# A two-block transformer forward on one core: first-layer score products over 128 rows, and the opening transfers in another order

## The chip, the cores and the metric

One core of a Trainium2 chip runs the whole program. The metric is the device time in microseconds (us). Engines: PE is TensorE (its matmuls), PEld its weight loads, DVE is VectorE, ACT ScalarE, POOL GpSimd, SP SyncE, which here only issues transfers.

## What is computed

The reference runs two blocks over 512 tokens of width 1024, in float32. The change lies in the first block. It projects the normed rows `hn` with `w_in` and has four groups of four attention heads, each head 64 wide; their results are gated, projected with `w_out` and added to `x`. The second block (sparse attention, a gated MLP mixer, a SwiGLU) follows.

```python
hn = rms_norm(x, norm_gain)
proj = jnp.einsum('btd,de->bte', hn, w_in)
...
o_fox = forgetting_attention(rms_norm(to_heads(fq, FOX_HEADS), fox_qk_gain[0]), ...)
o_moba = moba_attention(rms_norm(to_heads(mq, MOBA_HEADS), moba_qk_gain[0]), ...)
o_sb = stick_breaking_attention(to_heads(sq, SB_HEADS), ...)
o_swa = swa_sink_attention(rms_norm(to_heads(wq, SWA_HEADS), swa_qk_gain[0]), ...)
...
return x + jnp.einsum('bte,ed->btd', y, w_out)
```

Every head needs the product of its queries and keys, a contraction over 64 numbers: `jnp.einsum('bhqd,bhkd->bhqk', q_i, k)`. The biases that depend on the distance of a query and a key come from tables (`rel_bias`, `rel_bias_2`) by a one-hot product.

## The kernel before

One timeline, a Python list that `make_timeline` writes, sets the order on all engines: each engine walks the list and emits its share of each step, with semaphores between them. The large projections are cut into chunks of at most 512 columns and eight steps of 128 contraction rows. Such a step is called a tick here; it is twelve matmuls (`product`, L1038: four token tiles by three partial products, since each operand is split into a high and a low part). ACT makes the high part of a weight tile (L1425), POOL the low part (L2154), four tiles ahead, in a ring of six. A float32 matmul stands in the profile as two records, an fp32r one as one.

Between the ticks `at(tick, ...)` and `flush` put the attention of the first block: `("S", name, h, g)` is a group of score products of head `h` (PE L1246, then DVE L1933, then the exponential on ACT L1559), `T` its transposes (L1261), `O` its product with the values (L1286), `Z` and `F` the same for the stick-breaking heads `sb` (L1299, L1314). Behind each score segment of `fox` and `sb` stands a 128-row bf16 matmul that adds the mask (L1251, L1301). `fox` has its scores from tick 18, `moba` from 31, `sb` from 45, `swa` from 60.

Queries and keys reach the score products through `qa`, `qb` and `qt`: DVE squares and sums a token tile (L1835 to L1837), POOL takes the power (L2177), DVE scales (L1842), PE transposes four blocks into the bank `TR` (L1214), and DVE copies that bank, two heads per 128 rows, into `qkT1` (L1861, or L1858 for `sb`). The bank `TR` is also where `T` writes, and `T` waits until the copy has freed it. A head's q is then the upper or the lower 64 rows:

```python
e = 64 * (h % 2)
return qkT1[e:e + 64, KINDS1[name] % 2, h // 2, :]
```

The opening: SP loads the first tile of `x`, the gain, the identity, five table transfers, the other tiles of `x`, two groups of weights (L886, groups of four weight tiles, each loaded when the group two before it is split), and then twelve small constants. DVE and POOL multiply by the gain (L1675, L2162), PE transposes (L1112), ACT and DVE make the high and low parts (L1441, L1770). The distance rows (L1047, `distance_rows`) are four float32 matmuls of 33 rows by 8 columns of weights against 512, 512, 512 and 128 columns, and stand before the transposes of the last token tile. `rows_out` on DVE (L1655) copies them out; `setup` (L1637 to L1645) converts the constants. SP stores them, replicates each to 128 rows in DRAM and reads them back skewed as biases.

Of the kernel before, what the change touches and what calls it, by code (L numbers as in the profile page):

```python
# [14 lines left out]
P = 128  # L15
# [125 lines left out]
def make_timeline(first, n_slots):  # L141
# [129 lines left out]
    for t in range(NT):  # L271
# [122 lines left out]
    for t in range(NT):  # L394
        tl.extend([("sq", "ffn", t), ("yf", t, 0), ("ms", "ffn", t), ("yf", t, 1), ("post", "ffn", t)])
    return tl


def hybrid_two_block_kernel(nc, a, c, out):
# [22 lines left out]
    with ExitStack() as ctx:  # L422
# [35 lines left out]
        qkT1 = at("qkT1", 161, [2, 4, SEQ])  # L458
# [8 lines left out]
        hot_cmp = at("hot_cmp", 179, [1024])  # L467
        rows = at("rows", 199, [1664])
# [116 lines left out]
        hot_r = sem("cmp_hots_copied")  # L585
        gains_done = sem("gains_multiplied")
# [13 lines left out]
        qn_done = sem("qk_normed")  # L600
        s_cmp = sem("cmp_hots_landed")
# [260 lines left out]
        def _(sp):  # L862
# [53 lines left out]
            def replicate_rows():  # L916
                sp.wait_ge(s_rows, 48)
                for lo, n in ((0, 4), (8, 8)):
                    for h in range(lo, lo + n):
                        sp.dma_start(rep_d[h], rows_d[h:h + 1, :].broadcast_to([P, 640])).then_inc(s_rep, 16)  # L920
# [7 lines left out]
            def load_bias1():  # L928
                sp.wait_ge(s_rep, 16 * 16)
                for h in range(4):  # L930
                    skewed(bias_moba[:, h, :], rep_d, h, 512, 640).then_inc(s_bias1, 16)
                for h in range(4):
                    skewed(bias_swa[:, h, :], repb_d, h, 256, 384).then_inc(s_bias1, 16)

            def load_bias2():

                sp.wait_ge(tr_in, nth["F", 3, 2] + 1)
                sp.wait_ge(sp_done, 4)
                for h in range(8):
                    skewed(bias_t5[:, h, :], rep_d, 8 + h, 512, 640).then_inc(s_bias2, 16)  # L940

            def load_hot_cmp():

                sp.wait_ge(sc_out, nth["S", "moba", 3, 2] + 1)
# [45 lines left out]
            def load_gain(n, name, pre):  # L990
# [12 lines left out]
                index["out1", 0, 0]: [lambda: load_gain(0, "norm_mix_pre_2", (gx_pool, NT)),  # L1003
# [1201 lines left out]
```

## Time and profile before

| | us |
|---|---|
| median of 3 runs | 1060.28 (1058.92 to 1060.36) |
| the profiled execution | 1059.54 |
| its span, from the first to the last instruction | 1057.4 |
| PE busy | 998.2 (94% of the span) |
| DVE, ACT, POOL busy | 435.3, 390.3, 382.8 |
| chain that ended last, PE's share | 80% |

The profiled execution is 0.74 us below the median and 2.1 us above its own span, which is what lies before and after the first and last instruction. A row of the trace gives the start, the time, the engine, the line of the kernel, the operation, its tile, how many instructions were merged in the row, and in brackets how long the engine sat idle before and what ended that. For PE the form begins with rows*columns of the array, as 64*128. Matmuls overlap: what a matmul costs is read from one start to the next.

### The profile page before, as it was taken

What the parts mean: (1) busy time and instruction counts of PE and PEld (TensorE: products, weight loads), DVE (VectorE), ACT (ScalarE), POOL (GpSimd) and SP (SyncE); (2) the same over time, 40 slices, a digit from 0 to 9 for tenths busy, and PEclk for the clock granted to TensorE, in tenths of its full rate; (3) what the DMA queues carried; (4) which work ended last, traced back from release to release, by engine and by line L of the source; (5) the groups of instructions that cost most, each with busy time, mean ns of one, the idle gap of its engine ahead of it and who ended that gap; (6) DMA issues with size and microseconds to landing.
All of it is one profiled execution on the core that took longest, in us unless ns stands there. A gap on an engine that the chain in (4) does not pass through costs nothing.

```text
span 1057.4 us, 13172 instructions
## 1 busy us (share of the span) xinstructions
PE 998.2 (94%) x5055; PEld 816.7 (77%) x5055; DVE 435.3 (41%) x931; ACT 390.3 (37%) x724; POOL 382.8 (36%) x303
## 2 busy tenths in 40 slices
PE   6979999999998999989988889899999999999997
PEld 3867777776877887888877888787888888888886
DVE  3462532339655544527467756371000110132224
ACT  4232333334735324224546444443222232333332
POOL 4461422235121533223230004444544354444442
PEclk9989999999999999999999999999999999999999
DMA  6652121122115242052130002124332323223222
GB/s 227 194 186 49 41 80 41 40 81 65 41 40 199 81 155 67 22 179 81 40 120 21 1 2 80 41 80 111 125 114 80 120 80 102 98 82 117 80 80 80
DMA packets 69309, 93.06 MB, mean 88 GB/s; under 512 B 10348, under 2 KB 47761, under 8 KB 69248
## 3 DMA queue, kind: packets, MB, share of 16 engines
q1 hardware_dynamic: 69248, 92.23, 27.3%
q8 instruction: 40, 0.66, 0.3%
q14 instruction: 21, 0.17, 0.1%
HBM read 90.09 MB, written 6.85 MB: 92 GB/s over the span
## 4 chain that ended last, share of the span: by engine, by line
PE 80%; DVE 10%; issue 3%; DMA 2%; ACT 2%; POOL 1%; SPq 0%; DVEq 0%; POOLq 0%; ACTq 0%
PE psum L1038 60%; PE psum L1286 5%; PE psum L1246 4%; PE psum L1261 2%; PE psum L1338 1%; PE psum L1112 1%; POOL st L2177 1%; PE psum L1214 1%; DVE prob L1933 1%; DMA r_scratch<-st 1%; PE psum L1314 1%; DMA RAW<-in_w_gate_up_dram 1%; DVE sq L1835 1%; PE psum L1299 1%; DVE R L1741 1%
## 5 line engine op out<-in xcount | busy, mean ns | idle before, releaser
L2154 POOL TENSOR_TENSOR WR<-RAW,WR 128x512 fp32r<-128x512 f32 (+2 forms) x268 | 346.4, 1303 | 570.4 <-ACT WR L1425 570.4
L1038 PE MATMUL psum<-WR,XT 128*128 128x512 f32 (+2 forms) x2160 | 502.3, 388 | 6.0 <-DVE st L765 2.7
L1038 PEld LDWEIGHTS psum<-WR,XT 128*128 128x128 f32 x2160 | 390.7, 190 | 82.5 <-issue 3.7
L1425 ACT ACTIVATE WR<-RAW 128x512 fp32r<-128x512 f32 (+2 forms) x268 | 159.5, 614 | 239.1 <-PE psum L1038 220.6
L1038 PE MATMUL psum<-XT,WR 128*128 128x512 f32 x1056 | 243.3, 392 | 4.3 <-POOL WR L2154 2.5
L1038 PEld LDWEIGHTS psum<-XT,WR 128*128 128x128 f32 x1056 | 199.5, 189 | 46.4 <-POOL WR L2154 3.0
L1559 ACT ACTIVATE prob<-prob,st 128x512 f32<-128x512 f32 (+2 forms) x112 | 58.9, 546 | 160.4 <-DVE st L1933 146.7
L1286 PE MATMUL psum<-ones_up,probT 128*128 128x128 f32 x536 | 77.3, 285 | 12.5 <-DVE R L1963 8.5
L1783 DVE TENSOR_TENSOR gated<-psum,r_bc 128x512 f32<-128x512 f32 x22 | 14.2, 686 | 176.0 <-PE psum L1038 160.9
L1286 PEld LDWEIGHTS psum<-ones_up,probT 128*128 128x128 f32 x536 | 68.6, 196 | 21.1 <-issue 13.7
L2177 POOL TENSOR_TENSOR st<-st 128x8 f32<-128x8 f32 (+2 forms) x27 | 30.4, 1126 | 92.9 <-DVE st L1837 38.8
L2124 DVE TENSOR_TENSOR XT<-actT,XT 128x512 fp32r<-128x512 f32 x22 | 28.3, 1285 | 83.6 <-ACT XT L1616 83.6
L1261 PE MATMUL psum<-ident_sb,prob 128*128 128x128 f32 x268 | 44.4, 281 | 6.3 <-DVE qkT L1861 1.6
L1770 DVE TENSOR_TENSOR XT<-psum,XT 128x512 fp32r<-128x512 f32 x40 | 26.5, 687 | 47.3 <-ACT XT L1441 47.2
L1933 DVE CUSTOM_DVE_ANT_0 prob<-psum,bias_t 128x512 f32<-128x512 f32 (+1 forms) x64 | 29.9, 486 | 31.2 <-PE psum L1246 28.9
L1441 ACT ACTIVATE XT<-psum 128x512 fp32r<-128x512 f32 x40 | 22.8, 593 | 52.6 <-PE psum L1112 52.6
L1261 PEld LDWEIGHTS psum<-ident_sb,prob 128*128 128x128 f32 x268 | 31.2, 143 | 11.2 <-DVE probT L830 5.6
L1511 ACT ACTIVATE gated<-gated 128x512 f32<-128x512 f32 x22 | 13.4, 631 | 59.7 <-DVE gated L1783 59.7
L1246 PE MATMUL psum<-qkT 64*128 64x256 f32 (+3 forms) x96 | 32.8, 442 | 0.0
L830 ACT ACTIVATE probT<-psum 128x512 f32<-128x512 f32 (+2 forms) x52 | 25.1, 482 | 20.1 <-PE psum L1261 19.9
L1112 PE MATMUL psum<-ident_sb,R 128*128 128x128 f32 x128 | 21.5, 312 | 8.5 <-DVE R L1675 8.4
L830 DVE COPY probT<-psum 128x512 f32<-128x512 f32 x28 | 19.3, 690 | 18.4 <-PE psum L1261 14.3
(216 smaller groups left out, 777.9 us busy)
## 6 DMA issues: line engine op xcount, KB each, us to landing
RAW<-in_w_gate_up_dram SPq DMA_DIRECT2D x44, 512.0 KB, 4.8
RAW<-in_w_in_dram SPq DMA_DIRECT2D x16, 1024.0 KB, 5.2
RAW<-in_w_down_dram SPq DMA_DIRECT2D x11, 1024.0 KB, 4.8
RAW<-in_w_out_dram SPq DMA_DIRECT2D x8, 1024.0 KB, 5.1
RAW<-in_w_in_dram SPq DMA_DIRECT2D x12, 512.0 KB, 4.6
rep_scratch<-rows_scratch SPq DMA_DIRECT2D x12, 320.0 KB, 7.6
R<-in_x_dram SPq DMA_DIRECT2D x4, 512.0 KB, 5.5
x_again<-in_x_dram SPq DMA_DIRECT2D x1, 2048.0 KB, 7.9
```

Of the source, the lines that this page charges most:

```text
L830: (eng.activation(dst, src, ACT.Copy) if eng is nc.scalar else eng.tensor_copy(dst, src)).then_inc(tr_out, 1)
L1038: last = pe.matmul(outp, stationary(x), moving(y), start=start and n == 0, stop=stop and n == 2)
L1112: last = pe.transpose(bank[:, P * q:P * q + P], src[:, P * k:P * k + P], ident[:, :])
L1246: last = pe.matmul(bank[:, col:col + m * P], q_of(name, h)[:, P * i:P * i + P], k_of(name, h, x)[:, P * j:P * (j + m)], start=x == 0, stop ...
L1261: last = pe.transpose(TR[:, P * q:P * q + P], buf[:, P * q:P * q + P], ident[:, :])
L1286: last = pe.matmul(OB[:, P * i:P * i + P].rearrange("p (x n) -> p x n", x=2), probT[:, at_:at_ + P], ones_and_v(name, h, j + b), start=b = ...
L1425: act.activation(WR[:, s % RING, 0, 0:w], RAW[:, g % 2, q, 0:w], ACT.Copy).then_inc(w_hi, 1)
L1559: last = act.activation(buf[:, col:col + m * P], buf[:, col:col + m * P], ACT.Exp, bias=nm[:, sl + n:sl + n + 1], scale=-1.0)
L1933: last = dve.tensor_tensor_reduce(buf[:, col:col + m * P], SC[nth[step] % 2][:, col:col + m * P], bias_of(name, h, i, m), 1.0, 3e38, ALU.a ...
L2124: dve.tensor_tensor(XT[:, kt % 8, 1, :], actT[:, kt, :], XT[:, kt % 8, 0, :].bitcast(F32), ALU.subtract).then_inc(act_lo, 1)
L2154: pool.tensor_tensor(WR[:, s % RING, 1, 0:w], RAW[:, g % 2, q, 0:w], WR[:, s % RING, 0, 0:w].bitcast(F32), ALU.subtract).then_inc(w_lo, 1)
L2177: pool.tensor_tensor(dst, src, half[:, 0:1].broadcast_to([P, n]) if n > 1 else half[:, 0:1], ALU.pow).then_inc(r_ready, 1)
```

## The change

Each first-layer q head gets its own 128-row tile in which the rows of the head that shares its transposed block are zero (`QK1[name]`, slots 0 to 3 for q, 4 and 5 for k as before). A score product then contracts over all 128 rows of the k block. Three memsets on POOL write the zeros (`zero`), and the copy out of `TR` becomes three DVE instructions. In the opening the identity stands before the gain, and the tables are loaded behind the first two weight groups; the distance rows move behind the third tick of the first chunk and are computed in fp32r, from a rounded copy of the one-hots and from tables in a high and a low part, which makes eight fp32r matmuls where there were eight float32 records. Rows are replicated in DRAM in five portions, spread over the first projection, instead of at once. `hot_cmp` is loaded later, next to `x_again`.

```diff
 def make_timeline(first, n_slots):
...
-            tl.append(("rows",))
...
-    tl.append(("rows_out",))
     for c in range(len(CHUNKS1)):
         for k in range(KD):
             flush(8 * c + k, "in1", c, k)
+            if (c, k) == (0, 2):
+                tl.extend([("hots",), ("rows",), ("rows_out",)])
+            if (c, k) in ((0, 5), (2, 2)):
+                tl.append(("zero", ("fox", "moba")[c // 2]))
...
+    tl.insert(tl.index(("qa", "swa", 0)), ("zero", "swa"))
...
-        qkT1 = at("qkT1", 161, [2, 4, SEQ])
+        qk_fox = at("qk_fox_and_sb", 161, [6, SEQ])
+        qk_moba = at("qk_moba", 72, [6, SEQ])
+        qk_swa = at("qk_swa", 173, [6, SEQ])
+        QK1 = {"fox": qk_fox, "moba": qk_moba, "sb": qk_fox, "swa": qk_swa}
...
         def q_of(name, h):
-            e = 64 * (h % 2)
             if name in KINDS1:
-                return qkT1[e:e + 64, KINDS1[name] % 2, h // 2, :]
+                return QK1[name][:, h, :]
...
         def k_of(name, h, x=0):
-            e = 64 * (h % 2)
             if name in KINDS1:
-                return qkT1[e:e + 64, KINDS1[name] % 2, 2 + h // 2, :]
+                return QK1[name][:, 4 + h // 2, :]
...
-                index["in1", 1, 1]: [store_rows],
-                index["in1", 2, 0]: [replicate_rows],
-                index["in1", 2, 1]: [load_bias1],
+                index["in1", 2, 0]: [store_rows],
+                index["in1", 3, 0]: [replicate_moba],
+                index["in1", 3, 1]: [load_bias_moba],
                 index["in1", 4, 0]: [load_small2],
+                index["in1", 4, 1]: [replicate_band],
+                index["in1", 5, 0]: [load_bias_swa],
+                index["in1", 5, 1]: [lambda: replicate_full(8)],
+                index["in1", 6, 1]: [lambda: replicate_full(12)],
...
             sp.dma_start(R1[:, 0, :], x_v[:, 0, :]).then_inc(s_x[0], 16)
+            sp.dma_start(ident[:, :], c["ident"]).then_inc(s_ident, 16)
             bcast(gain[0][:, :], a["norm_gain"], D).then_inc(s_gain, 16)
-            sp.dma_start(ident[:, :], c["ident"]).then_inc(s_ident, 16)
-            load_tables()
...
                 load_group(g)
+                if g == 1:
+                    load_tables()
...
-                pe.wait_ge(s_tab, 80)
-                pe.wait_ge(setup_dve, 1)
-                for n, (bank, table) in enumerate(((SC[0], tab1), (SC[1], tab1), (TR, tab2), (OB, tab2))):
+                pe.wait_ge(hots_rounded, 1)
+                for n, (bank, table) in enumerate(((SC[0], tab1_parts), (SC[1], tab1_parts), (TR, tab_parts), (OB, tab_parts))):
                     lo, hi = (0, 512, 1024, 1536, 1664)[n:n + 2]
-                    pe.matmul(bank[0:8, 0:hi - lo], table[0:33, :], hots[0:33, lo:hi], start=True, stop=True).then_inc(tab_done, 1)
+                    for x in range(2):
+                        last = pe.matmul(bank[0:8, 0:hi - lo], table[0:33, 8 * x:8 * x + 8], hots_r[0:33, lo:hi],
+                                         start=x == 0, stop=x == 1)
+                    last.then_inc(tab_done, 1)
...
                 if what == "hots":
+
+                    dve.wait_ge(s_tab, 80)
+                    dve.tensor_copy(hots_r[0:33, :], hots[0:33, :])
+                    for parts, table in ((tab1_parts, tab1), (tab_parts, tab2)):
+                        link(dve.tensor_copy(parts[0:33, 0:8], table[0:33, :]))
+                        last = dve.tensor_tensor(parts[0:33, 8:16], table[0:33, :], parts[0:33, 0:8].bitcast(F32), ALU.subtract)
+                    last.then_inc(hots_rounded, 1)
...
-                        for part in range(2):
-                            dst = qkT1[:, kd % 2, 2 * part:2 * part + 2, tok]
-                            src = TR[:, 256 * part:256 * part + 256].rearrange("p (q n) -> p q n", q=2)
+                        q_k = TR.rearrange("p (x q n) -> p x q n", x=2, q=2)
+                        by_head = QK1[name][:, 0:4, tok].rearrange("p (q e) n -> p q e n", e=2)
+                        parts = [(slice(0, 64), by_head[0:64, :, 0, :], 0), (slice(64, 128), by_head[64:128, :, 1, :], 0),
+                                 (slice(0, 128), QK1[name][:, 4:6, tok], 1)]
+                        for own, to, part in parts:
...
+                if what == "zero":
+
+                    name = step[1]
+                    if name == "fox":
+                        pool.wait_ge(tab_out, 4)
+                        pool.wait_ge(setup_dve, 3)
+                    elif name == "moba":
+                        pool.wait_ge(gx_done, nth["gx", "in1", 3, 0] + 1)
+                        pool.wait_ge(sq_done, NT)
+                    else:
+                        pool.wait_ge(sc_out, nth["S", "moba", 3, 2] + 1)
+                    pool.memset(QK1[name][:, 0:4, :], 0.0).then_inc(zeroed, 1)
+                    continue
```

How the rows stand on PE at the start of the program, before. `L1112` (in the changed kernel `L1134`) transposes the normed rows, `L1047` (`L1067`) are the distance rows, `L1038` (`L1058`) the projection:

```order
L1112 MATMUL psum<-ident_sb,R_53 128x128 x24
L1047 MATMUL psum<-hots,st 8x512 x3
L1047 MATMUL psum<-hots,st 8x128
L1112 MATMUL psum<-ident_sb,R_53 128x128 x8
L1038 MATMUL psum<-WR,XT 128x512 x96
L1038 MATMUL psum<-WR,XT 128x260 x36
L1214 MATMUL psum<-ident_sb,qk_nat 128x128 x4
```

And in the changed kernel, the same place:

```order
L1134 MATMUL psum<-ident_sb,R_53 128x128 x32
L1058 MATMUL psum<-WR,XT 128x512 x36
L1067 MATMUL psum<-hots_r,tab_parts 8x512 x6
L1067 MATMUL psum<-hots_r,tab_parts 8x128 x2
L1058 MATMUL psum<-WR,XT 128x512 x60
L1058 MATMUL psum<-WR,XT 128x260 x36
L1236 MATMUL psum<-ident_sb,qk_nat 128x128 x4
```

The distance rows have moved from before the last eight transposes to behind the first 36 matmuls of the projection, and everything behind them is in the same order.

On DVE, at the second and third query tiles of `swa` (ticks 50 and 51), before. `L2005` takes an `F` out of `TR`, `L1979` a `Z` out of its bank, `L1987` is the long pass over a stick-breaking head, `L1861` the copy of the transposed q and k:

```order
L1979 COPY prob<-psum 128x256
L1987 SCALAR_TENSOR_TENSOR soft<-prob 128x1280
L1861 TENSOR_SCALAR qkT_72<-psum,st 128x2x128 x2
L1842 TENSOR_TENSOR qk_nat<-qk_nat,st 128x512
L1835 TENSOR_TENSOR sq<-qk_nat 128x512
L1836 TENSOR_REDUCE st<-sq 128x8
L1837 TENSOR_SCALAR st<-st 128x8
L2005 TENSOR_TENSOR prob<-prob,psum 128x512
```

In the changed kernel, where the copy is `L1897`:

```order
L2015 COPY prob<-psum 128x256
L2023 SCALAR_TENSOR_TENSOR soft<-prob 128x1280
L1897 TENSOR_SCALAR qk_swa<-psum,st 64x2x128 x2
L1897 TENSOR_SCALAR qk_swa<-psum,st 128x2x128
L1874 TENSOR_TENSOR qk_nat<-qk_nat,st 128x512
L1867 TENSOR_TENSOR sq<-qk_nat 128x512
L1868 TENSOR_REDUCE st<-sq 128x8
L1869 TENSOR_SCALAR st<-st 128x8
L2041 TENSOR_TENSOR prob<-prob,psum 128x512
```

Nothing changed its place; the two copies of 128 rows became two of 64 rows and one of 128, each of 256 elements per row. The same holds at all sixteen query tiles.

## Rows read from the trace of the kernel before

**Rows 1.** The page, busy time of each engine.
```profile
PE 998.2 (94%) x5055; PEld 816.7 (77%) x5055; DVE 435.3 (41%) x931; ACT 390.3 (37%) x724; POOL 382.8 (36%) x303
```

**Rows 2.** Busy time by stretch: stretch, length, busy (instructions) of PE, PEld, DVE, ACT, POOL, clock, DMA.
```profile
220.00:300.00 80.00, 76.05 (x381) 58.06 (x380) 57.00 (x78) 41.72 (x56) 26.67 (x18) 1.00 0.18 61
```

**Rows 3.** The timeline of PE at the first `moba` scores.
```profile
149.79 2.99 PE L1038 MATMUL psum<-WR,XT 128*128 128x512 f32 x12
152.71 1.12 PE L1246 MATMUL psum<-qkT 64*128 64x512 f32 x2
153.77 1.16 PE L1286 MATMUL psum<-ones_up,probT 128*128 128x128 f32 x8
```

**Rows 4.** The timeline of PE, a tick that is followed by a 128-row matmul.
```profile
215.02 3.00 PE L1038 MATMUL psum<-WR,XT 128*128 128x512 f32 x12
217.86 1.05 PE L1286 MATMUL psum<-ones_up,probT 128*128 128x128 f32 x8
```

**Rows 5.** The timeline of PE, float32 matmuls of 128 rows and 256 columns.
```profile
585.25 1.03 PE L1394 MATMUL psum<-zv,wsT 128*128 128x256 f32 x4
586.11 1.05 PE L1286 MATMUL psum<-ones_up,probT 128*128 128x128 f32 x8
```

**Rows 6.** The timeline of all engines in the opening.
```profile
9.13 0.69 DVE L1675 TENSOR_TENSOR R<-R,gain 128x512 f32<-128x512 f32 x1 [2.39 <-DMA R<-in_x_dram]
14.74 5.71 PE L1047 MATMUL psum<-hots,st 33*8 33x512 f32 x8
15.35 2.17 ACT L1425 ACTIVATE WR<-RAW 128x512 fp32r<-128x512 f32 x4
20.39 1.97 PE L1112 MATMUL psum<-ident_sb,R 128*128 128x128 f32 x8
23.86 28.13 PE L1038 MATMUL psum<-WR,XT 128*128 128x512 f32 x132 [1.50 <-DVE XT L1770]
27.25 2.07 DVE L1655 TENSOR_SCALAR rows<-psum 8x512 f32<-8x512 f32 x4
33.87 0.26 DVE L1645 TENSOR_SCALAR st<-st 128x1 f32<-128x1 f32 x3
34.17 0.42 ACT L1425 ACTIVATE WR<-RAW 128x260 fp32r<-128x260 f32 x1 [2.09 <-PE psum L1038]
```

**Rows 7.** The timeline of DVE and PE at a `moba` query tile.
```profile
126.31 0.88 DVE L1861 TENSOR_SCALAR qkT<-psum,st 128x256 f32<-128x256 f32 x2
127.25 0.66 PE L1261 MATMUL psum<-ident_sb,prob 128*128 128x128 f32 x4 [0.52 <-DVE qkT L1861]
```

**Rows 8.** The timeline of DVE and PE at an `sb` query tile.
```profile
198.04 0.75 DVE L1858 TENSOR_SCALAR qkT<-psum 128x256 f32<-128x256 f32 x2
198.84 0.44 PE L1261 MATMUL psum<-ident_sb,prob 128*128 128x128 f32 x2
```

**Rows 9.** The timeline of PE and DVE in the stick-breaking stretch.
```profile
243.40 0.70 PE L1314 MATMUL psum<-soft_parts,suffix_sb 128*128 128x512 f32 x2 [0.84 <-DVE soft_parts L1998]
247.12 0.66 PE L1214 MATMUL psum<-ident_sb,qk_nat 128*128 128x128 f32 x4 [1.47 <-DVE prob L2005]
256.63 0.42 DVE L2005 TENSOR_TENSOR prob<-prob,psum 128x256 f32<-128x256 f32 x1 [0.95 <-PE psum L1314]
```

**Rows 10.** The timeline of POOL and DVE: a power, idle time, a low part, a memset.
```profile
50.26 1.66 POOL L2177 TENSOR_TENSOR st<-st 128x8 f32<-128x8 f32 x1 [6.69 <-DVE st L1837]
86.87 1.29 POOL L2154 TENSOR_TENSOR WR<-RAW,WR 128x512 fp32r<-128x512 f32 x1 [9.31 <-ACT WR L1425]
235.28 1.64 POOL L2177 TENSOR_TENSOR st<-st 128x8 f32<-128x8 f32 x1 [11.55 <-DVE st L1837]
411.88 0.91 DVE L1756 MEMSET cmp_bias<- 128x1024 f32 x1 [8.36 <-PE psum L1075]
```

**Rows 11.** Busy time by stretch, columns as in the second group, and a tick in it.
```profile
65.20:75.40 10.20, 7.52 (x24) 5.76 (x23) 5.73 (x16) 4.38 (x10) 6.15 (x5) 0.50 0.35 110
70.45 4.21 PE L1038 MATMUL psum<-WR,XT 128*128 128x512 f32 x9 [2.68 <-DVE st L765]
```

More of the change, by code:

```diff
@@ L914, in store_rows, with replicate_full, replicate_moba, replicate_band @@
                 sp.dma_start(rows_d[8:16, 0:640], rows[0:8, 1024:1664]).then_inc(s_rows, 16)
-            def replicate_rows():
+            def replicate_full(lo):
+                for h in range(lo, lo + 4):
+                    sp.dma_start(rep_d[h], rows_d[h:h + 1, :].broadcast_to([P, 640])).then_inc(s_rep, 16)
+            def replicate_moba():
                 sp.wait_ge(s_rows, 48)
-                for lo, n in ((0, 4), (8, 8)):
-                    for h in range(lo, lo + n):
-                        sp.dma_start(rep_d[h], rows_d[h:h + 1, :].broadcast_to([P, 640])).then_inc(s_rep, 16)
+                replicate_full(0)
+            def replicate_band():
                 for h in range(4):
@@ L942, in load_hot_cmp @@
             def load_hot_cmp():
-                sp.wait_ge(sc_out, nth["S", "moba", 3, 2] + 1)
+                sp.wait_ge(sc_in, nth["S", "swa", 3, 1] + 1)
                 sp.dma_start(hot_cmp[0:33, :], c["hot_cmp"]).then_inc(s_cmp, 16)
@@ L1529, in _ @@
                         act.wait_ge(gx_pool, NT)
+                        act.wait_ge(sc_in, nth["S", "moba", 3, 2] + 1)
                     if (phase, ch) == ("in2", 2):
@@ L1650, in _ @@
                 what = step[0]
+                if what == "hots":
+                    dve.wait_ge(s_tab, 80)
[4 more added lines that the diff above has]
+                    last.then_inc(hots_rounded, 1)
                 if what == "rows_out":
@@ L1794, in _ @@
                         dve.wait_ge(gx_pool, NT)
+                        dve.wait_ge(sc_in, nth["S", "moba", 3, 2] + 1)
                     if (phase, ch) == ("in1", 2):
@@ L1847, in _ @@
                     if name in KINDS1:
-                        kd = KINDS1[name]
+                        if t == 0 and name != "sb":
+                            dve.wait_ge(zeroed, nth["zero", name] + 1)
                         if t == 0 and name == "sb":
@@ L1852, in _ @@
                         if t == 0 and name == "swa":
-                            dve.wait_ge(sc_in, nth["S", "moba", 3, 2] + 1)
-                        for part in range(2):
-                            dst = qkT1[:, kd % 2, 2 * part:2 * part + 2, tok]
-                            src = TR[:, 256 * part:256 * part + 256].rearrange("p (q n) -> p q n", q=2)
+                            dve.wait_ge(sc_out, nth["S", "moba", 3, 2] + 1)
+                        q_k = TR.rearrange("p (x q n) -> p x q n", x=2, q=2)
[3 more added lines that the diff above has]
+                        for own, to, part in parts:
                             if name == "sb":
-                                last = dve.tensor_scalar(dst, src, QSCALE if part == 0 else 1.0, None, ALU.mult)
+                                last = dve.tensor_scalar(to, q_k[own, part], QSCALE if part == 0 else 1.0, None, ALU.mult)
                             else:
                                 gcol = 2 * {"fox": 0, "moba": 1, "swa": 2}[name] + part
-                                last = dve.tensor_scalar(dst, src, qk_gain[:, gcol:gcol + 1], None, ALU.mult)
+                                last = dve.tensor_scalar(to, q_k[own, part], qk_gain[own, gcol:gcol + 1], None, ALU.mult)
                     elif name == "q":
@@ L1924, in _ @@
                     if h == 0 and g == 0 and name in ("moba", "swa"):
-                        dve.wait_ge(s_bias1, 128)
+                        dve.wait_ge(s_bias1, 64 if name == "moba" else 128)
                     if h == 0 and g == 0 and name == "slc":
```

24 lines of the change are left out of this document (15 added, 9 removed).

## The prediction

> **What bounds the kernel now.** First the page: PE is busy 94% of the span, every other engine at most 41% [rows 1]. Next the stretches: in most of the first block PE hardly stops; in the stretch with the stick-breaking heads it is busy 76 of 80 us, and DVE, with 57 of 80, is the next engine [rows 2]. So a microsecond taken from PE's stream counts, except where PE already waits for DVE. Then the timeline of PE, read from start to start, for what a change of shape costs.
>
> **The score products.** A score on 64 rows of the array stands between matmuls on 128 rows. The two records of 512 columns begin at 152.71 and the next matmul at 153.77: 1.06 us [rows 3]. Four float32 records of 256 columns on 128 rows take 586.11 - 585.25 = 0.86 us, 0.215 each [rows 5], so two of 512 would take about 0.86. The visit costs 0.20 more inside. It also starts late: the tick before it takes 152.71 - 149.79 = 2.92 us, a tick before a 128-row matmul 217.86 - 215.02 = 2.84 [rows 3, 4], another 0.08. One excursion to 64 rows thus costs 0.28 us beyond its columns. The change makes all score products 128 rows and leaves columns and their number alone.
>
> How many excursions: each `fox` head has four segments, each followed by a 128-row mask matmul, so 16; `moba` three groups a head, 12; `sb` again four segments and masks, 16; `swa` two groups, 8. Together 52, at 0.28: 14.6 us, were PE the bound at each.
>
> It isn't at all of them. At 243.40 PE waits 0.84 us for `soft_parts` and at 247.12 1.47 us for `L2005`, and not before 256.63 does DVE wait for PE again [rows 9]: in this stretch a PE that comes earlier only waits longer. I take the stretch as wide as the DVE passes of the second and third `sb` heads around it, about 232 to 265 us, in which 8 excursions lie (four of the second head, four of the third), and count them as nothing. The last four of `swa` stand behind the last tick, where PE has little else to do while DVE works; of these I count two. That leaves 42 x 0.28 = 11.8. At eight query tiles what follows hangs on DVE's copy, which starts from the score's end and doesn't see the 0.1 us lost on leaving 64 rows: 0.8 less. **Term: -11.0.**
>
> Against this term speaks the Trainium skill, TensorE: Matmul & The Clock Gate, section Why this matters for your kernels: a matmul with few contraction rows takes as long as one with 128, and padding buys nothing. By that alone the term would be 0 and the sum that of rival (c). Its page TensorEngine Tiling (Array Packing), Key Properties, says that a change of the tiling mode drains the engine; by that the term stands, and the trace's 1.06 against 0.86 us sides with it.
>
> **The copy out of TR.** Two DVE instructions take 0.88 us (0.75 in `sb`) for 256 elements a row each [rows 7, 8]; a third of the same columns adds about 0.40 (0.35) if an instruction on half the rows takes as long as one on all, and nothing if it took half. In `moba` the transposes `T` wait 0.52 us for exactly this copy; in `sb` the copy ends at 198.79 and the transposes start at 198.84, so there is no cover either [rows 7, 8]. Late next are the transposes `T` and the tick behind them. The four `fox` copies lie in POOL's power and are free (without that cover 1.6); `moba` 4 x 0.40, `sb` 4 x 0.35, `swa`, where DVE is the bound, 3 x 0.40. **Term: +4.2** (bounds 0 and 6).
>
> **The opening.** Distance rows hold PE from 14.74 to 20.39; then eight transposes, ACT and DVE, and the projection starts at 23.86 [rows 6]. Without them the last transposes run at once, but ACT has its four high parts first, until 15.35 + 2.17 = 17.52, then the two copies, and DVE's two subtractions behind; these took 20.39 to 23.86 = 3.5 us in all with the transposes, of which I put 2.0 behind ACT's first copy when nothing waits in between, an estimate. That puts the start at 19.5. The loads: `x` is now issued five transfers earlier; DVE waited until 9.13 for its second tile [rows 6]. I take 0.7 us off, an estimate between 0 and the 2.39 that DVE was idle for that tile, and low in it, since the bytes ahead shrink less than the count of transfers. Start 18.8, so -5.0. The new distance rows are six fp32r matmuls of 512 columns and two of 128. A projection matmul of 512 takes 2.84 / 12 = 0.24 us [rows 4]; 6 x 0.24 + 2 x 0.06 = 1.5, and a loss of 0.1 at each of eight for the odd shape as in the scores gives 2.3 (bounds 1.5, and 5.7, the old price [rows 6]). **Term: -2.7.**
>
> Does PE wait for them? Three ticks end at 34.17 [rows 6] when started at 23.86, so now at 29.1. The tables must have landed, and DVE must have rounded 33 x 1664 (about 1.7 us at the memset's 0.91 for 1024 [rows 10]) before that; in the kernel before, `setup` used constants issued behind the weights at 27.25 + 2.07 = 29.3 [rows 6]. No wait, I take it, with little to spare; a wait would cost its own length.
>
> What carries on behind: `rows_out` 2.07, `setup` from 29.3 to 34.13 = 4.8 [rows 6], so in the new kernel 31.4 + 2.1 + 4.8 = 38.3. Only then may POOL clear `qk_fox`. A memset of 2048 columns isn't in the trace: DVE's rate gives 1.8 us, POOL's 1.29 for 512 [rows 10] gives 5.2. Behind it POOL has two low parts, at most 1.29 each, then the first `fox` power, wanted at 50.26 - 2.7 = 47.6 [rows 10]. With 5.2 it is through at 46.1. What stands behind the memset is the low parts, for which PE would wait, and the powers, for which DVE would. The `moba` memset meets 9.31 us idle, the `swa` one 11.55 [rows 10]. Counted nothing.
>
> The `fox` ticks behind are a chain of DVE and POOL that only shifts with the first chunk. Replication now spreads over the first projection, where groups land well before their split; the old burst held SP and made ACT wait, but PE wasn't waiting for that. `hot_cmp` moves behind the `swa` scores, to the place of `x_again`, and isn't used before the second block: nothing. Two DVE instructions less there are hidden in an idle stretch.
>
> **Sum.** -11.0 + 4.2 - 2.7 = -9.5. On the profiled execution's 1059.54 that is 1050.0, which I forecast; the median of before lies 0.7 higher, well inside the range.
>
> **The clock.** From 65.20 to 75.40 PE's granted clock was 0.50, its 1.2 GHz level; before that PE had been idle between the `fox` tiles, 2.68 us of it at 70.45 [rows 11]. Nine matmuls took 4.2 us there instead of 9 x 0.24 = 2.2. The new kernel comes to this place at another moment: losing this stretch gives 2 us, a second one costs 2. It goes into the range.
>
> **Rivals.**
>
> (a) PE's gain arrives whole: the DVE stretches have slack I don't see, the copies cost half. -14.6 + 2.1 - 3.7 = -16.2: 1043.3. For it: PE is 94% busy. Against it: the 1.47 us wait [rows 9].
>
> (b) DVE is the bound more widely than from 232 to 265, so half the excursions are lost and the copies cost 5: -7.3 + 5.0 - 2.7 = -5.0, so 1054.5, or a little above.
>
> (c) The change of shape costs nothing, the 0.28 is how the profile models starts: 0 + 4.2 - 2.7 = +1.5: 1061, no change. Against it: only ends are modelled, and I read starts; the tick ahead is longer too [rows 3, 4].
>
> (d) Slower: the memset on POOL is dear. With m us each, `fox` is late by m - 6.7 (38.3 + m + 2.6 against 47.6), `moba` by m - 9.3, `swa` by m - 11.5. It eats 9.5 and 2.1 more at m = 13.0, 6.4 ns per column; POOL's subtraction takes 2.5 [rows 10]. At m = 15: 8.3 + 5.7 + 3.5 = 17.5 against 9.5, so 1068.
>
> **How the numbers follow.** Forecast 0.60, (a) 0.16, (b) 0.12, (c) 0.06, (d) 0.04, and 0.02 for the tables landing late. Within 0.2% is 2.1 us, about what a measurement tells from no change. Forecast, (a) and (b) are faster: 0.88; same 0.06; slower 0.06. The forecast's own range is 1046 to 1054; with (a) at 1043.3 and most of (b) it is 1042 to 1056.
>
> **What the changed kernel's profile should show.** The first projection matmul at about 18.8; distance rows in about 2.3 us without a wait ahead of them; `moba` scores of 512 columns at 0.86 us from start to start and ticks ahead of them at 2.84; PE's wait for the copy at `moba` query tiles up from 0.52 to 0.92; the waits at 243 and 247 longer than 0.84 and 1.47; the second block of the same length. I am wrong if 128-row scores keep the 1.06 us, if memsets take over 8 us, or if PE waits for the rounded tables.

## The result, and the profile after

| | before | after |
|---|---|---|
| median, us (lowest to highest) | 1060.28 (1058.45 to 1061.68), 5 runs | 1052.95 (1049.76 to 1053.77), 5 runs |
| profiled execution, us | 1059.54 | 1053.14 |
| its span, us | 1057.4 | 1051.1 |

The ratio is 0.993, with a 95% interval of 0.9916 to 0.9944: 7.3 us faster. The forecast was 1050.0 with a range of 1042 to 1056, so the time lies in the range, 2.95 us above the forecast.

The page of the changed kernel, busy time of each engine, answers to [rows 1].

```profile
PE 982.6 (93%) x5055; PEld 822.5 (78%) x5055; DVE 437.3 (42%) x950; ACT 389.7 (37%) x724; POOL 390.1 (37%) x306
```

PE has the same number of matmuls and 15.6 us less busy time; the span fell by only 6.3. Some of PE's time has thus turned into waiting. The timeline of PE at the same `moba` score as in [rows 3]:

```profile
145.18 3.00 PE L1058 MATMUL psum<-WR,XT 128*128 128x512 f32 x12
148.02 1.02 PE L1270 MATMUL psum<-qk_moba 128*128 128x512 f32 x2
148.87 1.05 PE L1310 MATMUL psum<-ones_up,probT 128*128 128x128 f32 x8
149.68 0.71 PE L1058 MATMUL psum<-WR,XT 128*128 128x512 f32 x2
```

The tick ahead takes 2.84 us from start to start (2.92 before), the two records of 512 columns 0.85 (1.06 before). Next, the timeline of DVE and PE at a `moba` query tile, which answers to [rows 7]:

```profile
120.47 1.48 DVE L1897 TENSOR_SCALAR qk_moba<-psum,st 64x256 f32<-64x256 f32 x3
122.00 0.66 PE L1285 MATMUL psum<-ident_sb,prob 128*128 128x128 f32 x4 [1.13 <-DVE qk_moba L1897]
```

Three copies take 1.48 us where two took 0.88, and PE waits 1.13 us for them where it waited 0.52. The view of PE's waits (who was waited for: us in total, times, longest) has the sum of such waits, the `moba` tiles first and then those of `sb`:

```profile
PE psum L1285 <- DVE qk_moba L1897: 4.0, 4, 1.1
PE psum L1285 <- DVE qk_fox_and_sb L1894: 2.9, 4, 0.9
```

The same view of the kernel before has, for the `moba` tiles:

```profile
PE psum L1261 <- DVE qkT L1861: 1.6, 4, 0.5
```

The opening, which answers to [rows 6], and the first memset:

```profile
8.55 0.69 DVE L1706 TENSOR_TENSOR R<-R,gain 128x512 f32<-128x512 f32 x1 [7.47 <-DMA gain<-in_norm_gain_dram]
20.58 4.80 PE L1058 MATMUL psum<-WR,XT 128*128 128x512 f32 x13 [2.86 <-DVE XT L1801]
30.54 1.68 PE L1067 MATMUL psum<-hots_r,tab_parts 33*8 33x512 f32 x8
32.15 5.04 PE L1058 MATMUL psum<-WR,XT 128*128 128x512 f32 x21
36.43 1.81 POOL L2204 MEMSET qk_fox_and_sb<- 128x2048 f32 x1
```

The projection starts at 20.58 (23.86 before), the distance rows take 32.15 - 30.54 = 1.61 us without a wait ahead of them, and a memset takes 1.81 us. Last, the stick-breaking stretch, which answers to [rows 9]:

```profile
236.00 1.03 PE L1338 MATMUL psum<-soft_parts,suffix_sb 128*128 128x512 f32 x2 [1.98 <-DVE soft_parts L2034]
239.70 0.66 PE L1236 MATMUL psum<-ident_sb,qk_nat 128*128 128x128 f32 x4 [0.22 <-DVE prob L2041]
```

PE waits 1.98 us for `soft_parts`, where it waited 0.84, and then 0.22 for `prob`, where it waited 1.47.

### The profile page after: what moved, and what is told of

It is laid out like the page before. It is cut to its first block, busy times and chain, and to the rows that moved or that the text cites. A ratio compares the mean times of both kernels' runs of the same rounds, so it can differ in the third digit from the quotient of the medians.

```text
span 1051.1 us, 13200 instructions
## 1 busy us (share of the span) xinstructions
PE 982.6 (93%) x5055; PEld 822.5 (78%) x5055; DVE 437.3 (42%) x950; ACT 389.7 (37%) x724; POOL 390.1 (37%) x306
## 4 chain that ended last, share of the span: by engine, by line
PE 78%; DVE 12%; issue 4%; DMA 2%; ACT 2%; POOL 1%; SPq 0%; DVEq 0%; POOLq 0%; ACTq 0%
PE psum L1058 60%; PE psum L1310 4%; PE psum L1270 3%; PE psum L1285 3%; PE psum L1362 1%; PE psum L1134 1%; POOL st L2226 1%; DVE prob L1969 1%; DMA r_scratch<-st 1%; PE psum L1338 1%; PE psum L1236 1%; DMA RAW<-in_w_gate_up_dram 1%; DVE sq L1867 1%; DVE R L1999 1%; DMA gain<-in_norm_gain_dram 1%
## 5 line engine op out<-in xcount | busy, mean ns | idle before, releaser
L1058 PE MATMUL psum<-WR,XT 128*128 128x512 f32 (+2 forms) x2160 | 503.6, 388 | 7.0 <-DVE XT L1801 2.9
L1058 PEld LDWEIGHTS psum<-WR,XT 128*128 128x128 f32 x2160 | 391.5, 190 | 84.4 <-POOL WR L2190 3.2
L1058 PE MATMUL psum<-XT,WR 128*128 128x512 f32 x1056 | 243.9, 393 | 4.9 <-POOL WR L2190 3.1
L1058 PEld LDWEIGHTS psum<-XT,WR 128*128 128x128 f32 x1056 | 200.1, 190 | 47.3 <-POOL WR L2190 3.5
L1285 PEld LDWEIGHTS psum<-ident_sb,prob 128*128 128x128 f32 x268 | 31.6, 145 | 15.6 <-DVE qk_moba L1897 4.8
L1134 PE MATMUL psum<-ident_sb,R 128*128 128x128 f32 x128 | 20.7, 310 | 10.1 <-DVE R L1706 10.1
L1134 PEld LDWEIGHTS psum<-ident_sb,R 128*128 128x128 f32 x128 | 17.5, 160 | 12.8 <-issue 10.0
```

Of the source, the lines that this page charges most:

```text
L1058: last = pe.matmul(outp, stationary(x), moving(y), start=start and n == 0, stop=stop and n == 2)
L1134: last = pe.transpose(bank[:, P * q:P * q + P], src[:, P * k:P * k + P], ident[:, :])
L1285: last = pe.transpose(TR[:, P * q:P * q + P], buf[:, P * q:P * q + P], ident[:, :])
```

## The experiments

All start from the changed kernel. Medians are of 4 to 12 runs each. The kernel before was run beside them, with medians of 1059.97 to 1060.27.

### A square: two or three copies, 64 or 128 rows

**x1** takes 64-row slices of the new tiles.

```
 q_of:  return QK1[name][64 * (h % 2):64 * (h % 2) + 64, h, :]
 k_of:  return QK1[name][64 * (h % 2):64 * (h % 2) + 64, 4 + h // 2, :]
```

> The changed kernel, but each first-layer score product takes 64 rows of the new tiles again (three copies, zeros and opening stay). Theory: an excursion to 64 rows costs 0.385 us where PE is the bound; fox 16 at about 0.26 (a chain of powers stands beside them), moba 12 and half of sb's 16 at 0.385, two of swa: 12.7 us, so 1065; seen without that sum, as before with 4.8 for the third copy and -1.7 for the opening: 1063.4. Between 1062 and 1066, and scores of 512 columns in moba 1.06 us from start to start again. Rival (the shape costs nothing, the gain is in the opening and in how the stages fall): within 1 of 1053.

**x2** also stores q as before, two heads of a pair above each other, so that two copies do; of the change only the opening, the replication in portions and the memsets are left.

```
 parts = [(slice(0, 128), QK1[name][:, 0:2, tok], 0),
          (slice(0, 128), QK1[name][:, 4:6, tok], 1)]
 q_of:  return QK1[name][64 * (h % 2):64 * (h % 2) + 64, h // 2, :]
 k_of:  return QK1[name][64 * (h % 2):64 * (h % 2) + 64, 4 + h // 2, :]
```

> The opening alone: two copies of 128 rows each and scores on 64 rows as before the change; memsets and load order as after it. Theory: the opening gives 1.7 us by the start of the second chunk and all of it reaches the end: 1058.6. Rival 1 (the first block waits for DVE later and swallows it): 1060.3. Rival 2 (the opening is the larger part of the gain, the late DVE chains hide what scores give): 1055 or below.

**x3** has the two copies of x2 and 128-row products, so that a product sums the scores of two heads.

```
 q_of:  return QK1[name][:, h // 2, :]
```

> The changed kernel with q copied out in one instruction of 128 rows (two copies in all), both heads of a pair in one tile; a score product on 128 rows then sums the scores of two heads, which are not the reference's. Theory: the third copy costs 0.6 us at 8 query tiles (moba, sb), nothing in fox and swa: 4.8 less, 1048.2. Rival (as I forecast, 0.40 and 0.35, three of swa too): 4.2 less, 1048.8, not to be told from the first by time, but by the waits of T: 0.52 against 0.72 in moba. Rival 2 (copies are hidden, the waits only moved): 1053.

| us, median (lowest to highest) | 64 rows | 128 rows |
|---|---|---|
| two copies | x2: 1058.82 (1057.22 to 1061.10) | x3: 1048.64 (1048.32 to 1050.17) |
| three copies | x1: 1064.78 (1063.07 to 1066.86) | changed kernel: 1052.95 |

The shape is worth 10.2 us with two copies and 11.8 with three; the third copy costs 6.0 at 64 rows and 4.3 at 128. The opening alone gives 1060.27 - 1058.82 = 1.45; its ratio to the kernel before, 0.9989 (0.9977 to 1.0001), hardly leaves 1. Along the path before, x2, x3, changed kernel: -1.45 - 10.2 + 4.3 = -7.3.

The same PE instruction in two kernels shows where the time came from. In x2 (64 rows, two copies), PE's timeline:

```profile
67.55 3.91 PE L1058 MATMUL psum<-WR,XT 128*128 128x512 f32 x9 [2.19 <-DVE st L773]
123.59 0.66 PE L1285 MATMUL psum<-ident_sb,prob 128*128 128x128 f32 x4 [0.52 <-DVE qk_moba L1896]
141.87 0.66 PE L1285 MATMUL psum<-ident_sb,prob 128*128 128x128 f32 x4 [0.52 <-DVE qk_moba L1896]
206.47 0.66 PE L1285 MATMUL psum<-ident_sb,prob 128*128 128x128 f32 x4 [0.40 <-DVE qk_fox_and_sb L1893]
239.73 0.70 PE L1338 MATMUL psum<-soft_parts,suffix_sb 128*128 128x512 f32 x2 [0.83 <-DVE soft_parts L2033]
298.12 1.13 PE L1270 MATMUL psum<-qk_swa 64*128 64x256 f32 x4
```

In x3 (128 rows, two copies), the same six places:

```profile
69.02 3.91 PE L1058 MATMUL psum<-WR,XT 128*128 128x512 f32 x9 [2.21 <-DVE st L773]
121.64 0.66 PE L1285 MATMUL psum<-ident_sb,prob 128*128 128x128 f32 x4 [0.52 <-DVE qk_moba L1896]
138.74 0.66 PE L1285 MATMUL psum<-ident_sb,prob 128*128 128x128 f32 x4 [0.52 <-DVE qk_moba L1896]
199.20 0.65 PE L1285 MATMUL psum<-ident_sb,prob 128*128 128x128 f32 x4 [0.40 <-DVE qk_fox_and_sb L1893]
231.63 0.70 PE L1338 MATMUL psum<-soft_parts,suffix_sb 128*128 128x512 f32 x2 [1.98 <-DVE soft_parts L2033]
290.58 1.08 PE L1270 MATMUL psum<-qk_swa 128*128 128x256 f32 x4
```

x3 starts 1.47 later at the first place, and 1.95, 3.13, 7.27, 8.10 and 7.54 earlier at the next ones. So it gains 3.42, 1.18 and 4.14 us in the first three stretches, in which 12, 4 and 12 excursions lie: 0.29, 0.30 and 0.35 each, 0.31 in the mean. Then 7 excursions gain 0.83 net, because the wait for `soft_parts` grows from 0.83 to 1.98: the missing 1.15 us are that wait. Over the next 9, x3 loses 0.56; its granted clock is 0.66 from 230 to 240 us there, that of x2 1.00.

### Is the stretch behind it DVE's?

**x4** puts the eight products of the second and third `sb` heads on 64 rows again.

```
 if name == "sb" and h in (1, 2): both tiles by [64 * (h % 2):64 * (h % 2) + 64]
```

> The changed kernel, but the 8 score products of the second and third sb heads take 64 rows again. Theory (this stretch is DVE's, and PE that comes earlier only waits): within 0.7 of 1053, with PE's waits at 236 to 257 us shorter by what the scores take more. Rival (each excursion counts): 8 x 0.385 = 3.1 more, 1056.

1051.40 (1050.93 to 1052.90): not slower, 1.5 below the changed kernel and not 3.1 above it. PE's timeline of x4, and then of the changed kernel at the last place:

```profile
236.25 0.70 PE L1338 MATMUL psum<-soft_parts,suffix_sb 128*128 128x512 f32 x2 [1.13 <-DVE soft_parts L2034]
239.97 0.66 PE L1236 MATMUL psum<-ident_sb,qk_nat 128*128 128x128 f32 x4 [1.47 <-DVE prob L2041]
289.69 0.70 PE L1338 MATMUL psum<-soft_parts,suffix_sb 128*128 128x512 f32 x2 [1.60 <-DVE soft_parts L2034]
```

```profile
289.24 0.70 PE L1338 MATMUL psum<-soft_parts,suffix_sb 128*128 128x512 f32 x2 [1.61 <-DVE soft_parts L2034]
```

The wait of 1.98 is 1.13 here: what the products took more, PE waited less. Three of the eight excursions lie ahead of 236.25, where x4 is 0.25 us behind the changed kernel, no more than at the start of the stretch (the mask matmul behind the first `sb` scores starts at 216.03 against 215.77). The other five lie behind it, and from 236 to 289 us x4 loses (289.69 - 236.25) - (289.24 - 236.00) = 0.20 us. Nor does a slower PE show: between the first two places the changed kernel's took 3.70 us at a granted clock of 0.83 (230 to 240 us), x4's 3.72 at 1.00, and the difference is in the wait, 0.22 against 1.47. The 1.5 us by which x4 is faster lie outside the edit: behind 302 us, where the two kernels are alike, stretches at half clock fall differently, and what causes them isn't settled.

### What does a copy cost, and who can take it?

**x5** splits the k copy into its two row halves, so there are four copies.

```
 parts = [..., (slice(0, 64), QK1[name][0:64, 4:6, tok], 1),
               (slice(64, 128), QK1[name][64:128, 4:6, tok], 1)]
```

> The changed kernel with the k copy in two instructions of 64 rows each, so four copies a query tile instead of three, 64 rows or 128 alike. Theory (an instruction on 64 rows takes as long as one on 128, about 0.49 us from start to start, and moba's and sb's query tiles have no cover): four copies in 1.97 us, T's waits up by 0.49, 8 x 0.49 = 3.9, with swa's last tiles up to 5: 1057 to 1058. Rival (half the rows take half the time, or the cost of the third was the jump between row halves): within 1 of 1053.

1055.66 (1055.25 to 1057.33), 2.7 above the changed kernel and somewhat under what I expected (in the profiles, of which x5's is its slowest run, the starts of the same PE instructions move by 3.7 between 115 and 215 us). The mechanism is as expected: PE's wait at the first `moba` tile rises from 1.13 by 0.49, exactly one instruction. In x5:

```profile
120.49 1.98 DVE L1897 TENSOR_SCALAR qk_moba<-psum,st 64x256 f32<-64x256 f32 x4
122.52 0.66 PE L1285 MATMUL psum<-ident_sb,prob 128*128 128x128 f32 x4 [1.62 <-DVE qk_moba L1897]
```

**x6** gives the odd heads' rows to ACT, at the step's place in ACT's order.

```
+ act: QK1[name][64:128, odd heads, tok] <- TR[64:128, 0:256], scale = the gain
  dve: even heads; wait_ge(odd_copied, ...); k
```

> The changed kernel, but ACT copies the odd heads' q rows (64 to 127) out of TR while DVE copies the even ones; DVE then copies k. Theory: DVE has two copies in a row again, T waits 0.5 to 0.6 less at 8 query tiles, 4.0 to 4.8 less: 1048 to 1049. Rival (ACT comes late in its program order, or its copy is as slow as both of DVE's): DVE waits for ACT's copy ahead of k, T's waits stay above 0.8 in moba, 1052 to 1053; from 0.6 us of lateness at each tile on it decides, and beyond it is slower.

1061.12 (1058.67 to 1063.14): all that the change had given is gone. The timeline of x6 at a `swa` tile shows why:

```profile
245.86 1.27 ACT L1615 ACTIVATE soft<-soft 128x1280 f32<-128x1280 f32 x1
247.15 0.47 ACT L1456 ACTIVATE qk_swa<-psum,st 64x256 f32<-64x256 f32 x1
247.65 0.48 DVE L1919 TENSOR_SCALAR qk_swa<-psum,st 128x256 f32<-128x256 f32 x1 [4.03 <-ACT qk_swa L1456]
248.19 0.44 PE L1339 MATMUL psum<-soft_parts,suffix_sb 128*128 128x384 f32 x1 [3.34 <-DVE qk_swa L1919]
```

ACT copies in 0.47 us, but only behind its softplus chain, so DVE waits 4.03 us and PE 3.34. By the starts of the same PE instructions x6 is 1.7 us behind the changed kernel at 215 us and 9.4 at 290: most of it is lost in `swa`.

**x9** keeps ACT's copy to `moba` and `sb`, and puts it ahead of the exponentials of the same step.

```
+ act, ahead of step "S" if the next step is ("qt", "moba" or "sb", t): the copy
```

> As the run in which ACT copies the odd heads' rows, but in moba and sb alone (swa and fox keep three copies on DVE), and in ACT's order the copy stands ahead of the exponentials of the same step, not behind them. Theory (what cost 8 us there was ACT's place: in swa's tiles DVE waited 4.03 us at 247.65 for an ACT inside its softplus chain, and in moba the exponential of 0.51 us stood ahead): now DVE never waits, T's waits fall by about 0.5 at each of 8 tiles: 1049, between 1048 and 1050.5. Rival (two engines reading one bank, or DVE's wait for ACT's semaphore, eat the gain): 1052 to 1053. Rival 2 (the exponentials, 0.5 later, are what T waits for): 1053 or more.

1047.83 (1047.07 to 1048.20), 5.1 below the changed kernel; the starts of the same PE instructions move ahead by 4.2 us between 60 and 215 us. In its profile the projection also starts 2.07 us earlier (18.51), which the edit doesn't touch, and 1.1 us are lost again from 215 to 263. ACT and DVE now copy side by side:

```profile
118.43 0.47 ACT L1454 ACTIVATE qk_moba<-psum,st 64x256 f32<-64x256 f32 x1 [2.83 <-PE psum L1237]
118.43 0.99 DVE L1925 TENSOR_SCALAR qk_moba<-psum,st 64x256 f32<-64x256 f32 x2
119.48 0.33 PE L1286 MATMUL psum<-ident_sb,prob 128*128 128x128 f32 x1 [0.64 <-DVE qk_moba L1925]
```

**x10** drops the memsets: one DVE instruction reads TR's q columns twice and multiplies by a factor per row that is zero for the neighbour's rows.

```
+ dve.tensor_tensor(QK1[name][:, 0:4, tok] as [P, 2, 2, P],
+                   TR[:, 0:256] as [P, 2, (twice), P], q_mask as [P, 1, 2, 1], ALU.mult)
- two copies of 64 rows, three memsets
```

> The changed kernel without its memsets and with q copied out by one DVE instruction on all 128 rows: TR's two q columns are read twice and multiplied by a per-row factor (the gain for a head's own half, zero for its neighbour's), 512 elements a row, which writes the zeros too; k as before. Theory (an instruction costs a fixed part and its elements; 512 elements of TENSOR_TENSOR take 0.69 us elsewhere on this engine): 0.69 + 0.48 = 1.17 in place of 1.48, 0.3 less at 8 tiles and at three of swa's in the DVE chain: 2.4 to 3.3 less, 1050. Rival (an operand that is broadcast and one in PSUM make it 1 us or more): 1053 or above; the trace tells the one duration.

1047.52 (1046.61 to 1049.27), 2.5 under what I expected. The timeline:

```profile
118.81 0.69 DVE L1904 TENSOR_TENSOR qk_moba<-psum,st 128x512 f32<-128x512 f32 x1
119.42 0.48 DVE L1908 TENSOR_SCALAR qk_moba<-psum,st 128x256 f32<-128x256 f32 x1
119.95 0.66 PE L1285 MATMUL psum<-ident_sb,prob 128*128 128x128 f32 x4 [0.73 <-DVE qk_moba L1908]
```

The pair takes 1.09 us, since the second starts 0.61 behind the first, and PE's wait is 0.40 shorter than in the changed kernel, not 0.31; at the first `sb` tile it is 0.27 shorter (0.67 for 0.94). From 115 to 215 us the starts move ahead by 2.7, and by another 0.8 in DVE's stretch, from 215 to 263. A further 1.7 us of this profile lie ahead of 76 us, where the projection starts at 19.19 and not at 20.58; the opening transfers are the same in both, so I don't count them as the copy's.

### The opening

**x7** has the opening transfers in the order of the kernel before; **x8** only the gain ahead of the identity.

```
 x7: x0, gain, identity, tables, x1 to x3, weights
 x8: x0, gain, identity, x1 to x3, two weight groups, tables
 changed kernel: x0, identity, gain, x1 to x3, two weight groups, tables
```

> The changed kernel with the opening transfers in the order of the kernel before (x0, gain, identity, tables, x1 to x3, weights); the distance rows still come after the third tick. Theory: the gain lands late in the changed kernel because the three x tiles are issued right behind it and share the queues; here it lands at about 6.0 instead of 8.45, the first product with it starts at 6.1, x1 at about 9.1, and the projection starts 1 us earlier, about 19.5: 1052. Rival (the chain through ACT's copies ends at x3, whose landing sets the start): gain early, start as in the changed kernel, 1053; if the tables' transfers delay x3, up to 1 later.

> The changed kernel with the gain issued ahead of the identity and nothing else moved (tables still behind the first weights). Theory (it shares the queues with the x tiles behind it): the gain still lands after 7.8, and nothing changes: 1053. Rival (the identity ahead of it is what costs): the gain lands at about 6, the identity at about 6.2.

1052.63 (1050.78 to 1054.50) and 1051.61 (1050.10 to 1052.04). The first product with the gain and the projection's start in x8:

```profile
6.62 0.69 DVE L1706 TENSOR_TENSOR R<-R,gain 128x512 f32<-128x512 f32 x1 [5.54 <-DMA gain<-in_norm_gain_dram]
18.66 5.71 PE L1058 MATMUL psum<-WR,XT 128*128 128x512 f32 x13 [2.86 <-DVE XT L1801]
```

My theory (the `x` tiles behind the gain slow it wherever the identity stands) fell: with the gain first it is there at 6.6, not after 7.8. But one profile is not enough here. In the nine profiles of kernels with the changed kernel's load order that product starts between 6.40 and 8.69, the mean being 8.03; the 6.40 is x9's:

```profile
6.40 0.69 DVE L1730 TENSOR_TENSOR R<-R,gain 128x512 f32<-128x512 f32 x1 [5.32 <-DMA gain<-in_norm_gain_dram]
```

In the three with the gain ahead of the identity and the tables late (x8, x11, x12) it starts at 6.62 to 6.73, in x7 at 6.12. The projection's start follows it: it lies 12.0 to 12.1 us behind that product in eight of these thirteen profiles, 11.2 in four and 13.2 in x7, where the tables come between. So the order helps the landing, most likely; in time x8 is 1.3 us under the changed kernel, and its runs lie in part among those of it.

**x11** is x10 with the gain first, and **x12** puts everything together.

```
 x11 = x10 + gain ahead of identity
 x12 = x9 (ACT's copy in moba, sb) + masked copy in fox, swa + gain ahead of identity
```

> The masked copy together with the gain issued ahead of the identity. Theory (the two lie in different stretches and add): the gain's 1.3 us on top of the masked copy's, 1048.7, and the projection starts near 18.7. Rival (the start's gain is lost again in the first block's chains, as the clock falls elsewhere): as the masked copy alone.

> All that helped: ACT copies the odd heads' rows in moba and sb, ahead of its exponentials; fox and swa use the masked copy in DVE; only moba's tile is cleared by POOL; the gain is issued ahead of the identity. Theory (each edit lies in a stretch of its own): by the ledger of starts, ACT's copy gave 4.2 us between 115 and 215 us, the masked copy 2.7 there and 0.8 in the DVE stretch behind; so here 4.2 + 0.8 and up to 1.3 from the opening, 6.3 under the changed kernel's 1053: 1046.6, between 1045 and 1048. Rival (DVE is the bound behind 230 us, so what is gained ahead is waited away there): as the masked copy with the gain, 1047.2 or above; the ledger then shows more at 215 us than at 263.

x11: 1047.16 (1046.19 to 1048.58), ratio 0.9885 (0.9868 to 0.9901), the fastest, though x9, x10, x11 and x12 can't be told apart. x12: 1048.00 (1045.20 to 1049.18), not 1046.6. Up to 215 us it goes as expected: from 60 to 215 us the starts of the same PE instructions say that x12 gains 1.7 us more than x11. It loses 1.5 again by 263. Busy time by stretch (length; busy PE, PEld, DVE, ACT, POOL; clock; DMA) of x12 shows a lower clock there:

```profile
230.00:235.00 5.00, 3.24 (x14) 2.51 (x15) 4.90 (x9) 0.63 (x1) 2.85 (x2) 0.69 0.01 3
235.00:240.00 5.00, 5.00 (x18) 4.05 (x17) 4.32 (x7) 3.77 (x4) 2.84 (x3) 0.63 0.00 0
```

x11:

```profile
230.00:235.00 5.00, 2.76 (x17) 2.31 (x18) 4.90 (x9) 0.63 (x1) 2.84 (x2) 1.00 0.01 3
235.00:240.00 5.00, 4.69 (x24) 3.43 (x23) 4.93 (x9) 3.89 (x4) 2.85 (x3) 1.00 0.00 0
```

PE comes out of a wait of 1.98 us for `soft_parts` in both, and in x12 alone its granted clock then falls, to 0.69 and 0.63 in the mean of the two stretches, so part of each at the 1.2 GHz level: 18 matmuls where 24 ran. The tick behind the wait takes 4.50 us to the next start in x12 (235.13 to 239.63) and 2.85 in x11 (234.65 to 237.50), which is the whole loss. So the rival had the place right and the reason wrong: it is the clock there, not DVE.

## Why the prediction was right, point by point

**The shape, forecast -11.0.** Right in mechanism and size: 10.2 and 11.8 in the square. The price was forecast as 0.28 an excursion and is 0.31 in the mean of 28. It depends on what stands behind the visit. Where an `O` group follows, I had overlooked a third piece: the eight matmuls behind the 64-row visit take 0.91 us to the start of the next tick in the kernel before, now 149.68 - 148.87 = 0.81. So there the price is 0.21 + 0.08 + 0.10 = 0.39. In the kernel before, PE's timeline behind [rows 3] goes on with:

```profile
154.68 1.63 PE L1038 MATMUL psum<-WR,XT 128*128 128x512 f32 x6
```

Rival (c), that the shape costs nothing, is out: x1 and x2 are 11.8 and 10.2 slower than their partners. So what spoke for it in the Trainium skill (TensorE: Matmul & The Clock Gate, Why this matters for your kernels: a single matmul over 32 contraction rows takes as long as one over 128), and what I drew from it, that padding buys nothing, doesn't carry over to products that stand between others of 128 rows. The Trainium skill's page TensorEngine Tiling (Array Packing), Key Properties, where a change of mode drains the engine, agrees with the 0.39.

**DVE's stretch, forecast as worth nothing.** Right: of x4's eight excursions there three cost nothing by 236 us, and the other five 0.20 between 236 and 289. The wait at 236 took them, as forecast (1.98 for 0.84). The one at 247 went the other way (0.22 for 1.47), where I had expected it to grow: PE's lower clock between the two took what the second would have been, as x4 shows. DVE sets the second place, however PE gets there.

**The copy, forecast +4.2.** The sum is right by chance of two errors. A copy of 64 rows costs 0.60 at a `moba` tile and 0.55 at an `sb` tile (three take 1.30 us, where two took 0.75), not 0.40 and 0.35: the 0.88 us of two copies [rows 7] is one of 0.40 to the next start and one of 0.48 to its end, and I divided by two and rounded down; among half-row instructions the starts are 0.49 to 0.51 apart in `moba`. Eight tiles are then 4.6, and in both columns of the square the starts move by 4.6 us between 75 and 215 us. Behind that, in `swa`, where I had counted 1.2, nothing lasts: at 64 rows x1 loses 1.1 more against x2 by 265 us and has it back by 335, and at 128 rows the changed kernel's 4.6 against x3 are 3.4 by 345. At 64 rows x1 also loses 1.3 between 61 and 76 us, in `fox`, where no copy costs anything: its transposes and the products with `tri_sb` behind them fall in a stretch at the 1.2 GHz level. So the 6.0 and 4.3 of the medians are 4.6 with the clock's part in them; how large that is in the medians stays open.

**The opening, forecast -2.7.** The weakest step. The start was forecast at 18.8 and came at 20.58 in this profile, because of a step that I took from the count of transfers: I took 0.7 off for `x` issued earlier, and didn't ask when the gain would land. The first product with it came 2.5 us later than in the kernel before, whose opening has:

```profile
6.05 0.69 DVE L1675 TENSOR_TENSOR R<-R,gain 128x512 f32<-128x512 f32 x1 [4.97 <-DMA gain<-in_norm_gain_dram]
```

The distance rows, on the other hand, took 1.61 us, not 2.3. Behind the first chunk the changed kernel is 1.64 us ahead of the kernel before. Measured alone the opening gives 1.45 (-0.1 to 2.4 by its interval), but that isn't what it saved in the opening. In x2's profile the gain came earlier than in the changed kernel's (its first product starts at 7.33), the projection starts at 19.36, and PE is 2.88 us ahead behind the first chunk, as forecast. The kernel before, then x2:

```profile
53.31 0.63 PE L1214 MATMUL psum<-ident_sb,qk_nat 128*128 128x128 f32 x4 [1.32 <-DVE qk_nat L1842]
```

```profile
50.43 0.63 PE L1236 MATMUL psum<-ident_sb,qk_nat 128*128 128x128 f32 x4 [1.32 <-DVE qk_nat L1874]
```

From 84 to 334 us x2 is 3.65 ahead. Then one and the same tick, which no edit touches, takes 3.17 us in the kernel before, 4.52 in x2 and 4.32 in the changed kernel, in this order:

```profile
334.47 3.17 PE L1038 MATMUL psum<-WR,XT 128*128 128x512 f32 x12
```

```profile
330.82 4.52 PE L1058 MATMUL psum<-WR,XT 128*128 128x512 f32 x12
```

```profile
325.52 4.32 PE L1058 MATMUL psum<-WR,XT 128*128 128x512 f32 x12
```

The granted clock of the tick is 0.94, 0.62 and 0.66: in the last two more of it lies at the 1.2 GHz level. At the end x2's span is shorter by 1.1 us only. What the fp32r rows, the moved transfers and the spread replication are worth each was not run apart.

**Hidden work.** The memsets take 1.81 us, the lower bound of 1.8 to 5.2; the first one starts at 36.43, and PE doesn't wait for it. Rival (d) had no ground. `setup` needed 1.2 us (33.21 to 34.4), not 4.8: its casts of 128x128 to bf16 take 0.21 us here, and took up to 1.33 in the kernel before. POOL was idle beside them here and busy there; no run tests whether that is the reason. Rounding the one-hots took 1.01 us, where I had put 1.7 (the rate that I named gives 1.5).

**Sum.** -10.2 + 4.3 - 1.45 against -11.0 + 4.2 - 2.7: of the 2.2 us difference 1.25 is the opening's term and 0.8 the shape's, by the medians. The profiles tell when it was lost. Ahead of the tick shown above the changed kernel leads by 334.47 - 325.52 = 8.95 us, of 9.5 forecast; behind it by 7.80, and at the end by 6.3, the difference of the spans. So a sign that I had named, a second block of the same length, failed: behind that tick the program is 1.5 us longer than before. By ACT's rows most of that goes between 690 us, where the lead is 8.4 (690.11 against 681.67), and 758, where it is 6.3 (757.90 against 751.63); from 725 to 735 us the granted clock is 1.00 in the kernel before and 0.83 in the changed one. My range had 2 us for such stretches, the forecast nothing. These are single executions, and whether the median loses the same is not shown. Rival (b), 1054.5, came nearer to the number, but its mechanism (half of the excursions lost) isn't what happened: of the 28 up to 206 us none is lost.

## What to carry to other kernels

Read a change of shape from start to start, and one matmul further than seems needed: part of its price lies in the tick ahead of it and part in the group behind it. When an engine copies by row halves, each half costs a whole instruction; look for one instruction on all rows (here a factor per row that is zero), or for another engine, and then ask where in that engine's order the copy stands: x6 and x9, of which only x6 leaves `fox` and `swa` to ACT too, lie 13 us apart. Compare the starts of the same instructions along the whole program before you call a difference of medians the worth of an edit: here 1.1 to 1.4 us of a lead were gone in one tick that no edit touched. Where a transfer is moved, ask of each that stands behind it when it lands, and take several profiles before you believe a landing time.

## What the hardware showed that was not expected

- PE's clock falls towards the 1.2 GHz level behind the same 1.98 us wait in some kernels and not in others (0.63 against 1.00 at 235 to 240 us in x12 and x11), 1.5 us of difference; what decides it stays open.
- POOL's memset of 128 x 2048 float32 took 1.81 us, while its float32 subtraction of 512 columns takes 1.27 to 1.29.
- A gain row that is broadcast to 128 partitions landed between 6.3 and 8.6 us with one and the same order of transfers, in the profiles of nine kernels.
- ACT and DVE reading different row halves of one PSUM bank at once didn't slow each other in x9: 0.47 us for ACT beside DVE's first copy, as in x6, where ACT copied alone; DVE's pair takes 0.99. The copy of k, which reads all rows, waits for ACT's by a semaphore.
- DVE's next instruction starts 0.40 us behind a copy of 128 rows and 0.49 to 0.51 behind one of 64 rows with the same 256 elements a row (`moba` tiles).
